# Joint attention with its bands in another order, fetched deeper, and the merge in half rows

## What is computed

```python
for gi, (win, dd) in enumerate(DIL_GROUPS):
    o_g, lse_g = dilated_band_attention(q_gi, k_gi, v_gi, positions, rel_bias_gi, win, dd)
wts = jax.nn.softmax(jnp.stack(lses), axis=0)
o_b = jnp.einsum('gbsh,gbshc->bshc', wts, jnp.stack(outs)).reshape(B, S, D)
g_a, g_b = jnp.split(jax.nn.sigmoid(gates), 2, axis=-1)
x = x + gt1 * ((g_a * o_a + g_b * o_b) @ w_out)
```

## Time and profile before

| | us |
|---|---|
| median of 3 runs | 3754.58 (3750.47 to 3765.54) |
| profiled execution | 3753.37, span 3751.2 |
| TensorE busy in the span | 3237.6 (86%) |
| VectorE, ScalarE, Pool busy | 1318.9, 666.8, 365.9 |
| projection stage `proj2` | 1838 to 2400 |
| attention stage `second_attention` | 2408 to 2630 |

### The profile page before, as it was taken

The page is one execution under the profiler, slowest core; times in us unless marked ns, Lnnn a source line. Parts: engine busy times, 40 slices in busy tenths (PEclk is TensorE's granted clock), DMA queues, the critical chain, the costliest instruction groups (busy, mean ns, idle before and its releaser), DMA issues. The chain is left out here.

```text
span 3751.2 us, 42445 instructions
## 1 busy us (share of the span) xinstructions
PE 3237.6 (86%) x16212; PEld 1607.4 (43%) x16212; DVE 1318.9 (35%) x2919; ACT 666.8 (18%) x1382; POOL 365.9 (10%) x459
## 2 busy tenths in 40 slices
PE   6788599949968699809999999978779999999998
PEld 4445344423454344305444444565434444444344
DVE  5405211134162111153999951265331222112222
ACT  1115122121221122120010021244100110101011
POOL 1103111130001111121000000012100000000000
PEclk9889699969988799959999999989889999999999
DMA  6862499923001999634324342681569999999994
GB/s 228 246 220 88 154 358 360 359 79 98 1 1 58 340 343 349 221 114 155 135 101 128 116 163 101 230 308 35 220 273 422 407 407 405 422 407 406 406 422 202
DMA packets 282749, 889.53 MB, mean 237 GB/s; under 512 B 35760, under 2 KB 75008, under 8 KB 233488
## 3 DMA queue, kind: packets, MB, share of 16 engines
q1 hardware_dynamic: 250576, 798.11, 56.6%
q0 software_dynamic: 32064, 89.97, 6.7%
HBM read 806.97 MB, written 80.99 MB: 237 GB/s over the span
## 5 line engine op out<-in xcount | busy, mean ns | idle before, releaser
L2899 PE MATMUL ec_gu<-ec_ring,ec_xg 128*64 128x512 f32 x2048 | 454.6, 595 | 0.9 <-ACT ec_xg L3051 0.9
L231 PE MATMUL proj_ps<-xT,proj_w 128*128 128x512 f32 x992 | 435.3, 601 | 19.1 <-DMA proj_w<-in_na_w_in 14.9
L231 PE MATMUL proj_ps<-proj_w,xT 128*128 128x512 f32 (+2 forms) x896 | 356.7, 560 | 14.8 <-DMA proj_w<-in_w_in 14.8
L231 PEld LDWEIGHTS proj_ps<-xT,proj_w 128*128 128x128 f32 x992 | 190.9, 193 | 260.2 <-issue 238.8
L2899 PEld LDWEIGHTS ec_gu<-ec_ring,ec_xg 128*64 128x64 f32 x2048 | 142.0, 137 | 303.3 <-issue 303.3
L231 PEld LDWEIGHTS proj_ps<-proj_w,xT 128*128 128x128 f32 x896 | 170.8, 191 | 198.5 <-issue 154.0
L2928 PE MATMUL ec_yp<-ec_ring,ec_hT 128*64 128x512 f32 x1024 | 248.0, 635 | 0.0
L1152 PE MATMUL moe_gu_ps<-moe_w,moe_xg 128*64 128x512 f32 x1024 | 231.9, 606 | 17.8 <-ACT moe_xg L1267 17.8
L2093 DVE SCALAR_TENSOR_TENSOR proj_acc<-proj_hit,proj_row,proj_acc 128x128 f32<-128x128 f32 (+1 forms) x512 | 243.6, 548 | 4.8
L718 PE MATMUL mix_o<-mix_w,xT 128*128 128x512 f32 x384 | 174.1, 614 | 20.4 <-DMA mix_w<-in_w_out 20.4
L260 ACT ACTIVATE proj_o<-proj_ps 128x512 f32<-128x512 f32 (+1 forms) x120 | 70.8, 590 | 612.0 <-PE proj_ps L231 611.1
(11 more groups left out here) (498 smaller groups left out, 3662.9 us busy)
## 6 DMA issues: line engine op xcount, KB each, us to landing
ec_ring<-in_w_gate SPq DMA_DIRECT2D x128, 1024.0 KB, 9.4
ec_ring<-in_w_up SPq DMA_DIRECT2D x128, 1024.0 KB, 11.5
ec_ring<-in_w_down SPq DMA_DIRECT2D x128, 1024.0 KB, 11.4
moe_w<-in_exp_w_gate SPq DMA_DIRECT2D x32, 2048.0 KB
moe_w<-in_exp_w_up SPq DMA_DIRECT2D x32, 2048.0 KB, 14.6
moe_w<-in_exp_w_down SPq DMA_DIRECT2D x32, 2048.0 KB, 10.8
proj_w<-in_w_in SPq DMA_DIRECT2D x22, 2048.0 KB, 11.0
...
```

The lines of the kernel that those rows point to most:

```text
L231: mm = nc.tensor.matmul(bank[0:jb["op"], 0:jb["ow"]], lhs, rhs, start=(k == 0), stop=(k == nk - 1))
L2899: mm = nc.tensor.matmul(gu_ps[n][half, :], xg[:, k, c0:c0 + CAP], w[:, m * D_FF + n * 512:m * D_FF + (n + 1) * 512], start=(k == 0), stop= ...
```

## The change

The bands run in the order g = 1, 2, 0. The fetch ahead (`first`) takes queries and keys of six heads and the values of g = 1 and g = 2; the chunks of the projection stage are reordered to suit (g = 1 first, queries and keys of g = 0 last). In the attention stage each head's iteration also issues one value block of g = 0 (heads 0 to 6) or of the latent heads (10 to 13), and a bias tile of g = 2 or g = 0 (heads 8 to 19). Outputs of g = 1 and 2 are read back at heads 18 and 21. Both gates are fetched after the last band. The products with gate A move from VectorE's scaling to a Pool operation of their own, except for the last head. The merge steps start 7 steps earlier, blends are 8 of 512 columns instead of 4 of 1024, and Pool now multiplies two of the three bands. Buffers move: values of g = 2 take the place of the first band's bias accumulator, those of g = 0 lie in `xT` and `more`.

```diff
@@ -2238,39 +2239,43 @@
+ORDER = (1, 2, 0)
...
-        self.q, self.k = [sb(f"q{r}", [P, S]) for r in range(4)], [sb(f"k{r}", [P, S]) for r in range(4)]
-        self.bias = [sb(f"bias{r}", [P, 4 * 256]) for r in range(2)]
-        self.more = sb("v0", [P, len(self.starts) - NT, D])
-        self.v0 = [h[:, n, :] for n in range(NT)] + [self.more[:, n, :] for n in range(len(self.starts) - NT)]
+        self.q, self.k = [sb(f"q{r}", [P, S]) for r in range(self.R)], [sb(f"k{r}", [P, S]) for r in range(self.R)]
+        self.acc1 = sb("acc1", [P, DIL_H, BIAS_WIDTH[1]])
+        self.big = sb("big", [P, DIL_H * BIAS_WIDTH[0]])
+        self.acc0 = self.big[:].rearrange("p (h n) -> p h n", h=DIL_H)
+        self.v = {1: h[:], 2: self.big[:, 0:4 * D].rearrange("p (u n) -> p u n", u=4)}
+        self.x_T = x_T[:].rearrange("p (u a) s -> p u (a s)", u=4)
...
+        self.heads = [(g, h_) for g in ORDER + (3,) for h_ in range(DIL_H)]
-        self.q += [self.sb(f"q{r}", [P, S]) for r in range(4, self.R)]
-        self.k += [self.sb(f"k{r}", [P, S]) for r in range(4, self.R)]
-        self.bias += [self.sb(f"bias{r}", [P, 4 * 256]) for r in range(2, self.RB)]
-        self.v1, self.v2 = self.sb("v1", [P, 4, D]), self.sb("v2", [P, 4, D])
+        self.ga = self.sb("bias", [P, self.RB, 4 * 256])
+        self.bias = [self.ga[:, r, :] for r in range(self.RB)]
+        self.more = self.sb("more", [P, 4, D])
+        self.v0 = [self.x_T[:, n, :] for n in range(4)] + [self.more[:, n, :] for n in range(len(self.starts) - 4)]
+        self.o1, self.oa = self.sb("o1", [P, NT, D]), self.sb("oa", [P, NT, D])
...
@@ -2279,27 +2284,26 @@
         if m < DIL_H:
-            sp.dma_start(self.bias[r][:].rearrange("p (u n) -> p u n", u=4), self.b0[:, m, :, 64:64 + 256]).then_inc(self.b_in[r], 16)
+            sp.dma_start(self.bias[r][:, 0:4 * P], self.b2[m]).then_inc(self.b_in[r], 16)
         else:
-            sp.dma_start(self.bias[r][:, 0:4 * P], self.b2[m - DIL_H]).then_inc(self.b_in[r], 16)
+            sp.dma_start(self.bias[r].rearrange("p (u n) -> p u n", u=4), self.b0[:, m - DIL_H, :, 64:64 + 256]) \
+                .then_inc(self.b_in[r], 16)
         if g == 0:
-            for n, s in enumerate(self.starts):
-                sp.dma_start(self.v0[n], self.vs[0][s:s + P, :]).then_inc(self.v_in[0], 16)
+            sp.dma_start(self.v0[n], self.vs[0][self.starts[n]:self.starts[n] + P, :]).then_inc(self.v_in[0], 16)
         else:
-            for u in range(4):
-                sp.dma_start((self.v1, self.v2)[g - 1][:, u, :], rows(self.vs[g], u)).then_inc(self.v_in[g], 16)
+            sp.dma_start(self.v[g][:, n, :], dilated_views(g)[1](self.vs[g], n)).then_inc(self.v_in[g], 16)
     def first(self, sp):
         self.load_qk(sp, 0)
-        self.load_bias(sp, 0)
-        self.load_v(sp, 0)
         self.load_qk(sp, 1)
-        self.load_bias(sp, 1)
-        self.load_qk(sp, 2)
-        self.load_qk(sp, 3)
+        for u in range(4):
+            self.load_v(sp, 1, u)
+        for n in range(2, self.R):
+            self.load_qk(sp, n)
+        for u in range(4):
+            self.load_v(sp, 2, u)
@@ -2318,19 +2322,20 @@
-    og = [xT[:].rearrange("p (u a) s -> p u (a s)", u=U), h[:], bb.v1[:], bb.oa[:]]
+    og = [bb.v[2], bb.o1[:], h[:], bb.oa[:]]
...
-    LN, WEIGH, EXP, SHARE, BLEND, FINAL = M0 + 8, M0 + 9, M0 + 11, M0 + 12, M0 + 13, M0 + 25
-    blend_at = {BLEND + 2 * t: t for t in range(NT)}
+    LN, WEIGH, EXP, SHARE, BLEND, FINAL = M0 + 1, M0 + 2, M0 + 3, M0 + 4, M0 + 6, M0 + 24
+    halves = [(t, slice(4 * q, 4 * q + 4)) for t in range(NT) for q in range(2)]
+    blend_at = {BLEND + 2 * b: b for b in range(2 * NT)}
@@ -2376,39 +2381,37 @@
-                bb.load_bias(sp, 2)
-                bb.load_bias(sp, 3)
-                bb.load_qk(sp, 4)
-                bb.load_qk(sp, 5)
-                bb.load_v(sp, 1)
+                for m in range(RB):
+                    bb.load_bias(sp, m)
                 for n in range(3 * H + 2):
-                    g, h_ = heads[n]
                     sp.wait_ge(s_ready, last_of[n] + 1)
                     bb.load_qk(sp, n + R)
-                    if g in (0, 2) and (h_ < RB or g == 0):
+                    if H <= n < 3 * H - RB:
                         sp.wait_ge(max_ready, last_of[n] + 1)
-                        bb.load_bias(sp, h_ + RB + (H if g == 2 else 0))
-                    if n == 2:
-                        bb.load_v(sp, 2)
-                    if n == H + 1:
-                        sp.wait_ge(pv_done, 2 * H)
-                        for t in range(NT):
-                            sp.dma_start(bb.ga[t], gates[t * P:(t + 1) * P, 0:D]).then_inc(ga_in, 16)
+                        bb.load_bias(sp, n - H + RB)
+                    if n < len(bb.starts):
+                        bb.load_v(sp, 0, n)
+                    if H + 2 <= n < H + 6:
...
+                        c = n - H - 2
+                        sp.dma_start(v_mla[:, c, :], v_all[c * P:(c + 1) * P, :]).then_inc(v_in, 16)
+                    if n == 2 * H:
...
-                    if n == 2 * H:
...
-                    if n == 2 * H + 4:
+                    if n == 2 * H + 2:
                         back(1)
+                    if n == 2 * H + 5:
+                        back(2)
                     if n == 3 * H - 1:
                         sp.wait_ge(pv_done, M0)
                         for t in range(NT):
-                            sp.dma_start(bb.v2[:, t, :], gates[t * P:(t + 1) * P, D:2 * D]).then_inc(gb_in, 16)
-                        back(2)
+                            sp.dma_start(bb.more[:, t, :], gates[t * P:(t + 1) * P, D:2 * D]).then_inc(gb_in, 16)
+                        sp.wait_ge(max_ready, M0)
+                        for t in range(NT):
+                            sp.dma_start(bb.bias[t], gates[t * P:(t + 1) * P, 0:D]).then_inc(ga_in, 16)
@@ -2419,28 +2422,39 @@
-                for g in (1, 2):
-                    store(g, 0, g * H + 3)
-                    store(g, 1, g * H + 7)
+                for i, g in enumerate(ORDER[0:2]):
+                    store(g, 0, i * H + 3)
+                    store(g, 1, i * H + 7)
...
-                for t in range(NT):
-                    nc.gpsimd.tensor_tensor(by_head(og[0][:, t, :]), by_head(og[0][:, t, :]), share(t, 0), ALU.mult) \
-                        .then_inc(weighed, 1)
-                        pool.wait_ge(blended, t)
-                        nc.gpsimd.tensor_tensor(h[:, t - 1, :], h[:, t - 1, :], bb.v2[:, t - 1, :], ALU.mult)
...
+                pool.wait_ge(og_in[1], 16 * NT)
+                def gate(b):
+                    t, hs = halves[b]
+                    cut = slice(hs.start * P, hs.stop * P)
+                    if b == 0:
+                        pool.wait_ge(gb_in, 16 * NT)
+                    pool.wait_ge(blended, b + 1)
+                    return nc.gpsimd.tensor_tensor(h[:, t, cut], h[:, t, cut], bb.more[:, t, cut], ALU.mult)
+                for b, (t, hs) in enumerate(halves):
+                    for g in (0, 1):
+                        v = by_head(og[g][:, t, :])[:, hs, :]
+                        x = nc.gpsimd.tensor_tensor(v, v, lse[:, t, g, hs].unsqueeze(2).to_broadcast([P, 4, P]), ALU.mult)
+                    x.then_inc(weighed, 1)
+                    if b:
+                        gate(b - 1)
+                gate(len(halves) - 1)
                 nc.gpsimd.drain().then_inc(merged, 1)
                 for f in range(H - 1):
+                    if f == 0:
+                        pool.wait_ge(ga_in, 16 * NT)
+                    nc.gpsimd.tensor_tensor(bb.oa[:, :, cols(f)], bb.oa[:, :, cols(f)], bb.ga[:, :, cols(f)], ALU.mult)
+                    nc.gpsimd.drain()
...
@@ -2566,12 +2580,14 @@
-                    if s == M0:
-                        dve.wait_ge(ga_in, 16 * NT)
                     dve.wait_ge(pv_done, s + 1)
-                    if g == 3:
-                        V.scalar_tensor_tensor(bb.oa[:, us[0], cols(h_)], o_ps[s % 2][:, 0:P], rd[:, 0:1], bb.ga[us[0]][:, cols(h_)],
+                    if g == 3 and h_ == H - 1:
+                        if gi == 0:
+                            dve.wait_ge(ga_in, 16 * NT)
+                        V.scalar_tensor_tensor(bb.oa[:, us[0], cols(h_)], o_ps[s % 2][:, 0:P], rd[:, 0:1], bb.bias[us[0]][:, cols(h_)],
                                                ALU.mult, ALU.mult).then_inc(out_done, 1)
+                    elif g == 3:
+                        V.tensor_scalar(bb.oa[:, us[0], cols(h_)], o_ps[s % 2][:, 0:P], rd[:, 0:1], None, ALU.mult).then_inc(out_done, 1)
@@ -2604,17 +2620,18 @@
-                def blend(t):
-                    for g in (1, 2):
-                        if t == 0:
-                            dve.wait_ge(og_in[g], 16 * NT)
-                        v = og[g][:, t, :].rearrange("p (h d) -> p h d", d=P)
-                        V.tensor_tensor(v, v, lse[:, t, g, :].unsqueeze(2).to_broadcast([P, H, P]), ALU.mult)
```

(16 more changed lines are left out.)

46 lines of the change are left out of this document (19 added, 27 removed).

## The result

The changed kernel takes 3720.1 us (median of 7 runs, 3713.6 to 3730.6), the kernel before on the same chip 3750.5 (3743.5 to 3765.5): ratio 0.992, 95% interval 0.990 to 0.994. 30.4 us are gone; 3723 were predicted, and the time lies inside the range of 3713 to 3741. The profiled run was the quickest of the seven, 3713.6 us with a span of 3711.4.

What follows compares the result with a forecast made beforehand. A transfer was taken to bound the bands and VectorE the merge. Bands 17 - 2 = 15 us, latent heads 4 + 13 - 1.4, about 16: 31 us off the 3754.6 median gives 3723, range 3713 to 3741.

Steps and rivals of the forecast that it cites:

- flat quarter rate: Bands: 102 to 106 GB/s for seven slices means the third band's values load on four of 16 engines, delaying later loads.
- (a) fetch ahead: End of projection stage: the four-engine load moved there ends by 2400, hidden behind matmuls; cost taken as 0.
- (b) the steps: Bands: 16 steps of 2.96 us and 15 of 2.15 give 79.6 against 96.1 us; gain 16.5, taken as 17.
- (c) the queue: First band's bias tiles: bytes queued ahead leave them near their need; waits sum to 0 to 4 us, taken as 2.
- rival 1: Bands: the full queue replaces the old wait, tiles 3 to 10 us late; 5 to 15 us more; chance 0.15.
- Logarithms: Latent heads: ScalarE's 3.8 us wait for statistics goes, two table loads stay; gain 4 us.
- Blends: Merge: half rows, one product moved to Pool, cost TensorE nothing; the four old ones cost 13.2 us; gain 13.
- Tail: Stage end: the seventh head's separate Pool gate product delays the last addition; cost 1.3 to 1.5 us, 1.4 in the sum.
- 2: Rival, merge: Pool and VectorE shut each other out; 8 to 20 us more, 3731 to 3743; chance 0.09.
- 3: Rival, stage start: the fetch ahead sticks out past 2400 and holds the stage; 3 to 8 us more; chance 0.06.
- 4: Rival, bands: the clock stays at 1.2 GHz, 58 us lost, 3781 in all; chance 0.06 together with other slower ends.
- 5: Rival, bands: order and depth only move the wait to another head; 10 of 17 us left, 3735; chance 0.06.

Runs made afterwards that it cites:

- E1: Kernel before, only the third band's values loaded in 16 pieces of 32 rows instead of four loads; ratio 0.996, attention stage 207.8 us against 220.6.
- E2: Changed kernel with the third band's values loaded inside the attention stage, behind four bias tiles, in four loads; ratio 0.998, stage 216.2 us against 190.6.
- E3: Changed kernel with the third band's values loaded inside the attention stage, behind four bias tiles, in 16 pieces; ratio 0.995, stage 199.0 us.
- E4: Changed kernel with loads that only the latent heads need issued behind the bands' last bias tile; ratio 0.990, stage 184.8 us.
- E10: Changed kernel with E4's edit, plus the gate of the last two latent heads inside VectorE's scaling; ratio 0.988, stage 182.1 us.
- E11: E10 with Pool storing the third band's output in pieces of 32 rows; ratio 0.989, stage 181.7 us.
- E9: Changed kernel measured again, unedited; 3719.2 us, ratio 0.991 against the kernel before, stage 192.4 us.
- E6: Changed kernel with merge blends of whole rows instead of half rows; profiled only, 15 gaps between latent pairs 94.9 us against 87.4, stage 197.1 us.
- E7: Changed kernel with Pool's two products of each half row waiting until VectorE begins that half's blend; profiled only, stage 203.0 us against 190.6.

## Why the prediction held, and where its steps did not

The time lies inside the range because the two large readings were right, the load on a quarter of the engines and the merge that overfills VectorE. That the forecast of the bands came within 2 us was luck: two errors in it point opposite ways.

- **Which part matters.** The reading of the flat quarter rate was right. E1 takes 12.8 us with it alone, and E2 loses 25.6 when it is brought back. Order, depth and place together brought the bands 2.2 us more than E1's new shape alone, and E3 against E1 points to the place of the load for it, not to order or depth (the runs don't part them fully).
- **(a) fetch ahead**: predicted 0, and none shows. I put its end 8 us ahead of the stage (2400 against 2408); it was 2391 against 2399.
- **(b) the steps.** The predicted sum, 79.6 us for the last of 32 steps, rested on a miscount. 2508.96 in the earlier trace rows is step 30 and not 31: the first latent scores stand between the transposes of steps 30 and 31, and I took them for their end. With 14 short steps the sum is 16 x 2.96 + 14 x 2.15 = 77.5 against 96.1, a gain of 18.6 and not 16.5. E4 and E10 come out at 76.7 and 76.0, and E11, where no tile is late, at 75.6, 1.9 below the model: its first pitches are 2.2 us, TensorE's pace, before VectorE's 2.97 shows. So the two pitches hold, and the way the stage starts was left out.
- **(c) the queue**: predicted 2 us of waits, measured 7.7, and 8.6 in E9 (its waits for `band_bias` sum to 5.1; another of 3.4 at head 21 is put down to TensorE, whose scores had been ready since 2472.5, but it ends with the landing of that head's tile). In TensorE's time they cost 7.2 us, 82.8 against 75.6 in E11. The prediction's own sign of rival 1, more than 4 us of such waits at heads 16 to 23, was met. The byte count was good for the first tiles (0.0 to 1.1 us late), not for the last: the tile of head 21 came 3.9 us late and that of head 23 2.5. Their issues in SyncE's queue and VectorE's waits for them:

```profile
2460.64 0.73 SPq L2289 DMA_DIRECT2D band_bias<-bias  x1
...
2474.20 1.26 SPq L2289 DMA_DIRECT2D band_bias<-bias  x1
...
2473.04 0.69 DVE L2568 SCALAR_TENSOR_TENSOR att_s<-att_s_ps,band_bias 128x512 f32<-128x512 f32 x1 [3.88 <-DMA band_bias<-bias]
...
2484.16 0.69 DVE L2568 SCALAR_TENSOR_TENSOR att_s<-att_s_ps,band_bias 128x512 f32<-128x512 f32 x1 [2.53 <-DMA band_bias<-bias]
```

  I had allowed for the way back ahead of them, 2 us, but not for SyncE, whose issues stretch on a full queue (one of 3.6, one of 4.6, one of 4.9 us). The maxima that these two issues wait for were done at 2456.4 and 2464.4, so they went out 4 and 10 us late, and the tiles landed 12.3 and 9.9 us behind them. This error and the miscount nearly cancel: 15 predicted, 13.3 measured.
- **Logarithms**: predicted 4, measured 4.8 (by E1's gaps it would be 2.6). **Blends**: predicted 13, the excess of the four gaps in the kernel before is 13.2, and in the changed kernel none is left. The cost of Pool's products was mis-sized: 1.04 us each and not 1.45, because I halved 2.87, which itself was a product locked against VectorE (alone a whole row takes 1.89, E6). The gate product was 1.27 as against 1.2.
- **Tail**: predicted 1.4, measured 1.7 as the growth of TensorE's wait (0.83 to 2.50). In the table 1.0 of it stands in the last but one gap (7.07 for 6.07), into which the earlier `FINAL` moves one turning, and 0.7 behind the last pair.
- **Rivals.** 1 happened: tiles 2.5 and 3.9 us late at two heads, 5.8 us of the stage (E4). Its price was hidden because the steps gained more than I had counted. 2 is real (E7) but was avoided. 3 and 4 did not occur: the clock is 0.96 to 1.00 by window. 5 did not occur at its price either (the bands gained 13.3 us and not 10), though what order and depth add by themselves stays open.
